# Hybrid attention and convolution layer: small steps moved in the hand-written orders of ScalarE, VectorE and GpSimd ahead of the main loop

## The reference

```
h = rms_norm(x, norm_w)
proj = h @ w_in     # q, six k/v groups, gate logits, nsa_z, cv_h, cv_b, cv_c, cv_z
q = rope(rms_norm(q));  k_s, k_w = rope(rms_norm(.))
k_c = rope(rms_norm(compress(k_c)));  v_c = compress(v_c)
      # compress: blocks of 32 rows, stride 16: silu(flat @ w1 + b1) @ w2
o_nsa = (g0 * attn(q, k_c, v_c) + g1 * attn(q, k_s, v_s) + g2 * window_attn(q, k_w, v_w)) * silu(nsa_z)
o_conv = cv_b * conv_w3(cv_c * cv_h) * silu(cv_z)
out = x + concat(o_nsa, o_conv) @ w_out
```

## Time and profile before

| | us |
|---|---|
| median of 3 runs | 692.04 (692.0 to 692.44) |
| the profiled execution's own time | 692.04 |
| its span, first to last instruction | 690.2 |
| PE busy in the span | 666.5 (97%) |
| DVE busy | 478.2 (69%) |
| ACT busy | 379.8 (55%) |
| POOL busy | 194.2 (28%) |
| mean granted TensorE clock, as a share of full speed | 0.995 |

### The profile page before, as it was taken

One profiled execution on the slowest core, in us unless ns is written; L12 is line 12 of the kernel. 1 busy time (PEld: TensorE's weight loads), 2 busy tenths in 40 slices (PEclk: granted clock), 3 DMA queues, 4 the chain that ended last, 5 costly groups with the idle time before them and its releaser, 6 DMA issues.

```text
span 690.2 us, 10353 instructions
## 1 busy us (share of the span) xinstructions
PE 666.5 (97%) x3551; PEld 558.5 (81%) x3551; DVE 478.2 (69%) x1141; ACT 379.8 (55%) x880; POOL 194.2 (28%) x216
## 2 busy tenths in 40 slices
PE   6999999999999999999999999899799999999997
PEld 5889998888888888888777888787678887788875
DVE  4935989792746555776597776877677778777742
ACT  6744458553344354365554665566776656655641
POOL 3523204503423222332122322123852212211110
PEclk9999999999999999999999999999899999999999
DMA  8413202202111111110101100011411101001101
GB/s 315 132 53 109 58 5 61 63 1 77 46 47 32 46 31 32 47 30 16 32 16 30 32 21 27 0 62 48 137 61 47 46 31 59 35 30 47 47 30 62
DMA packets 19348, 36.30 MB, mean 53 GB/s; under 512 B 2784, under 2 KB 3680, under 8 KB 19296
## 3 DMA queue, kind: packets, MB, share of 16 engines
q1 hardware_dynamic: 19296, 35.63, 16.4%
HBM read 31.43 MB, written 4.19 MB: 52 GB/s over the span
## 4 chain that ended last, share of the span: by engine, by line
PE 88%; DVE 6%; ACT 2%; issue 2%; DMA 1%; SPq 0%; ACTq 0%; DVEq 0%
PE pf L1380 10%; PE pf L1381 10%; PE pf L1382 10%; PE tp L1667 8%; PE po L1647 5%; PE sc L1517 5%; PE sc L1516 4%; PE pj L1382 4%; PE pj L1381 4%; PE pj L1380 4%; PE po L1648 4%; PE sc L1380 3%; PE sc L1382 3%; PE sc L1381 3%; DVE ptl L1314 1%
## 5 line engine op out<-in xcount | busy, mean ns | idle before, releaser
L896 ACT CAST pth<-tp 128x512 fp32r<-128x512 f32 (+1 forms) x148 | 86.8, 587 | 126.3 <-PE tp L1667 125.6
L1295 DVE CUSTOM_DVE_ANT_0 sc<-sc,maskb 128x64 f32<-128x64 f32 (+8 forms) x192 | 102.7, 562 | 52.7 <-PE sc L1517 52.4
L1314 DVE TENSOR_TENSOR ptl<-tp,pth 128x512 fp32r<-128x512 f32 (+1 forms) x148 | 101.9, 689 | 46.4 <-ACT pth L896 45.4
L623 POOL TENSOR_SCALAR qp<-qp,precip,gate 128x64 f32<-128x64 f32 x64 | 43.7, 682 | 180.9 <-DVE precip L1285 180.8
L1667 PE MATMUL tp<-cst,qp 128*128 128x128 f32 (+1 forms) x592 | 89.3, 273 | 1.9 <-issue 1.0
L1380 PE MATMUL pf<-hh,fh 128*128 128x512 f32 x200 | 81.0, 405 | 1.6 <-DVE mixc L1254 0.8
L1667 PEld LDWEIGHTS tp<-cst,qp 128*128 128x128 f32 (+1 forms) x592 | 69.4, 138 | 11.9 <-issue 1.9
L1381 PE MATMUL pf<-hl,fh 128*128 128x512 f32 x200 | 78.4, 392 | 0.0
L1382 PE MATMUL pf<-hh,fl 128*128 128x512 f32 x200 | 78.2, 391 | 0.0
L583 POOL TENSOR_TENSOR fl<-fraw,fh 128x512 fp32r<-128x512 f32 x36 | 48.6, 1351 | 93.2 <-ACT fh L749 93.2
L574 POOL TENSOR_TENSOR wl<-qp,wh 128x512 fp32r<-128x512 f32 (+1 forms) x33 | 47.4, 1458 | 91.1 <-ACT wh L663 91.1
(11 more groups left out here) (240 smaller groups left out, 1559.6 us busy)
## 6 DMA issues: line engine op xcount, KB each, us to landing
fraw<-in_wside SPq DMA_DIRECT2D x36, 256.0 KB, 2.6
qp<-in_wpack SPq DMA_DIRECT2D x28, 256.0 KB, 3.2
wor<-in_wout SPq DMA_DIRECT2D x16, 256.0 KB, 3.0
xo<-in_x SPq DMA_DIRECT2D x16, 256.0 KB, 2.8
out<-xo SPq DMA_DIRECT2D x16, 256.0 KB, 2.0
mixc<-in_xcm SPq DMA_DIRECT2D x4, 512.0 KB, 7.3
xlow<-in_xcm SPq DMA_DIRECT2D x3, 512.0 KB, 6.6
qp<-in_wpack SPq DMA_DIRECT2D x5, 224.0 KB, 2.5
```

Of the source, the lines that this page charges most:

```text
L896: nc.scalar.copy(pth[ptn % 2][0:r, :], tp[tpn % 2][0:r, :]).then_inc(pth_ready, 1)
L1295: return V.tensor_tensor_reduce(row, row, mask, -1.0, -NEG, ALU.add, ALU.min, most)
L1314: V.tensor_tensor(ptl[ptn % 2][0:r, :], tp[tpn % 2][0:r, :], pth[ptn % 2][0:r, :].bitcast(F32), ALU.subtract).then_inc(tp_read, 1)
```

## The change

Three engines' lists change; PE's and SP's stay as they are, and no instruction is added or taken away.

- ACT: the cast of w2 (`w2h`) moves from ahead of the Q items to behind the KC weight casts. The root of x moves from between Q 6 and Q 7 to behind Q 7 and the first three KV1 weight casts. `hidden(0)` moves behind the four W1 weight casts. The cast of the third side half moves from the very end to stand with the first two, ahead of Z 3.
- DVE: the low part of w2 and two operations on `hnorm` (the norm weights) move from behind Q 3 to behind the KV0 items, ahead of `normalise_k(0)`. The reduction of Q 7 comes ahead of the reductions of x and their chain.
- POOL: `copy_queries(0)` comes behind the subtractions of all three first side halves, and waits for the end of Z 3 (`item_done`) where it waited for `hid_done` 2.

```diff
@@ POOL @@
             for e in range(NE):
                 entry_weights(e)
-            pool.wait_ge(hid_done, 2)
+            for h in range(3):
+                half_lo(h)
+            pool.wait_ge(item_done, first_item[E_Z + 1])
             pool.wait_ge(q_normed, 1)
             copy_queries(0)
-            for h in range(2):
-                half_lo(h)
             pool.wait_ge(kt_ready, 9)
             pool.wait_ge(cmp_done, 2)
             copy_last_keys(0)
             copy_last_keys(1)
-            half_lo(2)
@@ ACT @@
-            act.wait_ge(param_in, 80)
-            nc.scalar.copy(w2h[:, :, :], prm[:, P_W2:P_W2 + 128].rearrange("p (f d) -> p f d", f=2)).then_inc(w2_hi, 1)
-            for m in range(NT - 1):
+            for m in range(NT):
                 item(E_Q, m)
+            for p in pieces(E_KV1)[:3]:
+                weights(p)
             act.wait_ge(const_in, 16)
             act.wait_ge(x_sum, 1)
             root(S_X, NT, DM, x_std)
-            item(E_Q, NT - 1)
-            for p in pieces(E_KV1)[:3]:
-                weights(p)
...
             for p in pieces(E_KC):
                 weights(p)
+            act.wait_ge(param_in, 80)
+            nc.scalar.copy(w2h[:, :, :], prm[:, P_W2:P_W2 + 128].rearrange("p (f d) -> p f d", f=2)).then_inc(w2_hi, 1)
             act.wait_ge(q_sums, 1)
             root(0, 64, HD, head_std)
...
             for p in pieces(E_Z):
                 weights(p)
-            hidden(0)
             for p in pieces(E_W1):
                 weights(p)
+            hidden(0)
             item(E_Z, 0)
...
-            for h in range(2):
+            for h in range(3):
                 half_hi(h)
             item(E_Z, 3)
...
-            half_hi(2)
@@ DVE @@
-            for m in range(NT - 1):
+            for m in range(NT):
                 item(E_Q, m)
-                if m == 3:
...
...
-            item(E_Q, NT - 1)
             for m in range(NT):
                 item(E_KV0, m)
...
             V.tensor_tensor(raw_sums, raw_sums, rsq.unsqueeze(2).to_broadcast([P, NT, 8]), ALU.mult).then_inc(q_sums, 1)
+            dve.wait_ge(w2_hi, 1)
+            V.tensor_tensor(w2l[:, :, :], prm[:, P_W2:P_W2 + 128].rearrange("p (f d) -> p f d", f=2),
+                            w2h[:, :, :].bitcast(F32), ALU.subtract).then_inc(w2_ready, 1)
+            link(V.tensor_scalar(hnorm[:, 0, :], hnorm[:, 0, :], 0.125, None, ALU.mult))
+            tail = hnorm[:, 0:1, 2 * ROT:HD].to_broadcast([P, 3, HD - 2 * ROT])
+            link(V.tensor_tensor(hnorm[:, 1:4, 2 * ROT:HD], hnorm[:, 1:4, 2 * ROT:HD], tail, ALU.mult))
```

## The result

| | before | after |
|---|---|---|
| median, us | 692.24 (692.0 to 692.52, 4 executions) | 701.2 (698.59 to 701.75, 4 executions) |
| ratio | 1 | 1.0114 (95%: 1.0089 to 1.0141) |
| profiled execution, us | 692.04 | 699.91 |
| its span, us | 690.2 | 698.1 |
| its mean granted clock | 0.995 | 0.992 |

By the medians the kernel became 9.0 us slower; the forecast was 4.7, and 701.2 lies above the range, which ended at 699.2. Eight executions of after are on record, the four of the median among them. Their mean is 700.2 us, 7.9 more than before, and the ratio 1.0114 agrees with that and not with 9.0. The direction and the places were right. Two amounts were missing: a fall of the clock behind one of the new waits, and a longer wait at 490 us, far behind the change.

The account below looks back on a forecast made before the run. PE, busy 666.5 of 690.2 us, was taken as the bound, so only its waits count. Slips of 0.6 + 1.1 + 1.5 + 1.5 = 4.7 us on 692.04 gave 696.7 us, range 694.0 to 699.2.

Parts of the forecast that it names:

- Term 1: At L1400: the later root of x and DVE operations waiting for POOL make PE slip 0.6 us.
- Term 2: At KV1 item 4: moved w2/qnorm work delays the first key normalisation by 1.42 us; PE slips 1.1 us.
- Term 3: At compressed(0): PE waits 2.5 us, the second keys' old 0.9 wait goes; PE slips 1.5 us.
- Term 4: At L1508: query copies wait for POOL's third subtraction; PE slips 1.5 us.
- Rival (c): Second key normalisation stays 10.0 us long because DVE isn't freed; 700.9 us, chance 0.05.
- Rival (d): The table switch on ACT costs 1.4 us more than its row; 698.1 us, chance 0.05.
- rival (b): Clock falls behind the new 2.5 us wait, about 140 us, losing 2.1 us; 698.8 us, chance 0.11.
- the sentence that all later work keeps the shift: From 170 us on: all later work is released by PE or its dependents, so every row stands 4.7 us later.
- Rival (e): Wait at 488 us, if DMA-paced, shrinks and takes back up to 4.69 us; 692.0 or 691.1, chance 0.07.

Follow-up runs that it names:

- e_root: Kernel before with only the root of x on ACT and the reduction of Q 7 on DVE in their new order; 693.08 us, ratio 1.0014.
- e_wout: Kernel before with the loads of output weights 4 to 7 on SP ahead of the wait for f_done and the residual loads; 687.51 us, ratio 0.9929.
- e_wout_after: Changed kernel with the loads of output weights 4 to 7 on SP ahead of the wait for f_done; 692.78 us, ratio 1.0018.
- e_fill_wout: Changed kernel with output weights 4 to 7 loaded ahead of the f_done wait and ten spare matmuls ahead of compressed(0); 693.04 us, ratio 1.0012.

## Why the prediction was right in its four slips and wrong in its sum

**Term 1, the root of x, 0.6.** The idle time is 0.41, in after and alone. The waits for POOL came as told, two of DVE's small operations took 0.97 instead of 0.17:

```profile
56.45 0.97 DVE L972 TENSOR_SCALAR stat<-stat 128x8 f32<-128x8 f32 x1 [0.43 <-ACT stat L755]
```

**Term 2, w2 on DVE, 1.1.** Idle 1.11, slip 1.28. DVE waited 1.97 us for the copy and each of the three operations met a subtraction of POOL; the normalisation's L1127 stands at 87.19, 2.1 us behind its 85.08 in the earlier trace rows. Of that, 0.7 is the lag that the run had already from the first step, and 1.4 is what was told.

```profile
81.36 0.98 DVE L1090 TENSOR_TENSOR w2l<-prm,w2h 128x128 fp32r<-128x128 f32 x1 [1.97 <-ACT w2h L784]
82.27 1.27 DVE L1092 TENSOR_SCALAR hnorm<-hnorm 128x64 f32<-128x64 f32 x1
83.58 1.32 DVE L1094 TENSOR_TENSOR hnorm<-hnorm 128x144 f32<-128x144 f32 x1
```

**Term 3, hidden(0), 1.5.** Wait 2.34 for 2.5, old wait gone, slip without the clock 3.19 - 1.55 = 1.6. Both halves of the argument stand in the rows. DVE's small operations, 1.31 and 1.22 beside POOL, take 0.17 now that POOL has ended, and the large ones take 1.23:

```profile
141.69 0.17 DVE L975 SCALAR_TENSOR_TENSOR stat<-stat 128x16 f32<-128x16 f32 x1
141.90 0.17 DVE L976 SCALAR_TENSOR_TENSOR stat<-stat 128x16 f32<-128x16 f32 x1
142.10 1.23 DVE L1126 TENSOR_TENSOR qp<-qp,stat 128x1024 f32<-128x1024 f32 x1
```

Rival (c), a normalisation that stays 10 us long, is refuted by them. Rival (d), 1.4 us more for the switch of tables, is refuted too. The load lies bare now, as foreseen, and tanh starts 0.01 us behind its end:

```profile
137.97 0.62 ACT L662 CAST wh<-qp 128x512 fp32r<-128x512 f32 x1 [0.41 <-DMA qp<-in_wpack]
138.61 1.28 ACT L729 ACT_TABLE_LOAD   x1
139.90 0.31 ACT L729 ACTIVATE hid<-hid 128x128 f32<-128x128 f32 x1
```

The drain of 1.38 us that the Trainium skill ("ScalarE: Activation LUTs", section "What ACT_TABLE_LOAD costs") puts beside each load does not appear in these rows.

**Term 4, POOL's copies, 1.5.** Idle 1.61. The copies start when the third subtraction ends, at 170.85, and PE's turns 0.94 later.

The four slips are 0.4 + 1.3 + 1.6 + 1.6 = 4.9 us, for 4.7 forecast.

**The step that failed first is the clock, which the sum put at nothing** and left to rival (b). The mechanism was named there, the place too, and the price, 2.1 us, lies between the two that the rows show, 1.55 and 3.0. What was wrong was its chance, 0.11, drawn from the wait being half as long as the one at 488 us. Of the three traces with this wait unfilled, two have the fall. Filling the wait brings 2.5 us by the means and 3.6 by the medians with the old order on SP, more than the 1.55 of the profiled execution, but only 0.6 by the means with the new order. One row of before could not tell it: the trace had a single long wait, so there was no row of a wait of 2.4 us with or without a fall behind it.

**The second is the sentence that all later work keeps the shift.** Rival (e) asked only whether the wait at 488 us would shrink. It was longer, by 0.5 to 1.6 us, in after and in the six variants with the old order on SP. In after SP was released exactly as much later as PE; in e_root it was released earlier, and the wait was longer too.

In the profiled execution of after the account closes: 0.3 us were there ahead of the first new wait, the four slips with their small change are 5.2, the fall at compressed(0) is 1.55, the late wait is longer by 1.6, and the shorter half-rate stretch behind it gives back 0.7. That is 7.9 us, the difference of the spans. By the medians the difference is 1.1 us larger; two of the four executions of that median were at half rate for 14 to 17 us by their mean clock, against 10.2 in the trace, and where is not on record.

**The range** was built from single rivals. Forecast and (b) together gave 698.8 and were at its edge; a third surplus on top, which no case held, put the time outside. Rival (e) has a slip of its own: the four terms already count the 0.9 us wait as gone, so its 691.1 counts it twice and 692.0 was the floor. The 0.02 for a faster kernel rested on it.

**What stays open.** Why the data take 3.8 us from the first issue to the first cast in the kernel before (4.0 in a second trace) and 4.5 to 5.8 in the variants was not found. What is shown is that it is a wait for loads issued behind f_done: in e_wout and e_wout_after, where they leave earlier, PE's wait is 1.2. Whether their number in one bunch matters was not tested. And why the clock falls at compressed(0) in one execution and not in the next, and until 144.6 or until 147.8 us, no row tells.

## What to carry to other kernels

Where the matrix engine is busy for 97% of the span, a reordering elsewhere is a set of races, and each can be placed from rows to some 0.2 us; but a new idle time on that engine like the 2.3 us here should be given its clock price too, at a chance of about even, unless some work can be put in the gap. Profile more than one execution of a kernel before a difference of half a microsecond far from the change is given a cause. Ask of every long wait that is already there, however far behind the change, what it is waiting for: a bunch of loads issued behind a late semaphore is both a gain that waits to be taken (4.9 us here) and a place where a changed kernel can lose more than the change itself costs. Issue such loads ahead of the wait as soon as their buffers are free.

## What was not expected of the hardware

- Ten additional matmuls, 2.4 us of work, made the kernel 2.5 us faster by the means and 3.6 by the medians (0.6 and nothing where the loads had been moved), with the granted clock at 1.00 where it had been 0.55.
- Behind idle times of nearly the same length, 2.34, 2.44 and 2.47 us, at the same place of the program, PE ran at half rate for 3.3 us, not at all, and for 6.4 us.
- The clock also fell behind a wait of 1.19 us, with a wait of 0.82 us shortly ahead of it (e_wout_after, 492.6 to 496.0), and did not behind the same two waits of 0.82 and 1.17 us in e_wout and e_fill_wout.
- The same loads took 3.8 us to the first cast in one kernel, 4.7 in another in which they were issued 0.3 us earlier, and 5.8 in a third in which they were issued 7 us later.
